# One layer with 32 routed experts on one core: results scattered to their token's place, and the down product put off behind the next gate product

## The reference, cut to what matters

```python
h2 = rms_norm(x, norm_ffn)                     # 320 tokens x 1024
grp = argmax(h2 @ w_rg + b_rg)                 # one of 4 groups
top_val, top_idx = top_k(logit_e of grp, 2)    # two of its 8 experts
y_e = (silu(xb @ w_gate[e]) * (xb @ w_up[e])) @ w_down[e]   # xb: tokens of expert e
x = x + sum over the two experts of weight * y_e
```

## Time and profile before

| | us |
|---|---|
| median of three executions | 1235.9 |
| the profiled execution | 1233.81 |
| its span | 1232.3 |
| PE busy | 1174.5 (95%) |
| DVE busy | 298.2 (24%) |
| ACT busy | 239.2 (19%) |
| POOL busy | 85.2 (7%) |

### The profile page before, as it was taken

The page is one execution under the profiler, slowest core; times in us unless marked ns, Lnnn a source line. Parts: engine busy times, 40 slices in busy tenths (PEclk is TensorE's granted clock), DMA queues, the critical chain, the costliest instruction groups (busy, mean ns, idle before and its releaser), DMA issues.

```text
span 1232.3 us, 14577 instructions
## 1 busy us (share of the span) xinstructions
PE 1174.5 (95%) x5878; PEld 647.5 (53%) x5878; DVE 298.2 (24%) x743; ACT 239.2 (19%) x497; POOL 85.2 (7%) x128
## 2 busy tenths in 40 slices
PE   6999999999899999999996999999999999899796
PEld 3477876555577777777644433333433333344243
DVE  1131033446623222131215111111111111012314
ACT  2021011334411111320012111111111111111135
POOL 0020040000112110000000000000000000001000
PEclk9999998999998888899996999999999999999998
DMA  9950194102023335355414799999999999999901
GB/s 330 274 175 1 69 166 143 47 23 69 29 81 106 107 133 200 114 205 205 156 64 190 300 414 415 414 415 415 415 414 415 414 415 415 412 415 417 334 12 43
DMA packets 77329, 288.98 MB, mean 235 GB/s; under 512 B 21587, under 2 KB 25916, under 8 KB 56732
## 3 DMA queue, kind: packets, MB, share of 16 engines
q1 hardware_dynamic: 54972, 256.67, 53.8%
q0 software_dynamic: 21920, 31.15, 8.7%
q10 hardware_dynamic: 384, 0.41, 0.1%
HBM read 276.55 MB, written 15.62 MB: 237 GB/s over the span
## 4 chain that ended last, share of the span: by engine, by line
PE 43%; DMA 13%; DVE 2%; issue 1%; ACT 1%; SPq 0%; POOL 0%; ACTq 0%; DVEq 0%
PE ps L1022 14%; DMA late<-in_w_exp_up_dram 9%; PE ps L526 8%; PE ps L1038 6%; PE ps L582 4%; PE ps L999 4%; DMA ring<-in_w_exp_up_dram 3%; PE ps L1029 2%; PE ps L1007 1%; PE ps L547 1%; PE ps L946 1%; PE ps L589 1%; PE ps L563 0%; PE ps L517 0%; PE ps L810 0%
## 5 line engine op out<-in xcount | busy, mean ns | idle before, releaser
L1022 PE MATMUL ps<-ring,reg_xh 128*64 128x512 f32 x512 | 151.1, 603 | 8.2 <-DMA late<-in_w_exp_up_dram 4.5
L1022 PE MATMUL ps<-late,reg_xh 128*64 128x512 f32 x336 | 149.2, 597 | 2.9 <-DMA reg_k<-in_w_exp_up_dram 1.7
L1853 DVE TENSOR_TENSOR reg_xh<-reg_xh,ps 64x512 f32<-64x512 f32 x32 | 22.1, 691 | 350.5 <-ACT reg_xh L1343 350.5
L1022 PEld LDWEIGHTS ps<-ring,reg_xh 128*64 128x64 f32 x512 | 49.6, 139 | 105.9 <-issue 103.6
L999 PE MATMUL ps<-reg_xh 128*64 128x512 f32 x384 | 89.6, 601 | 1.7 <-DVE reg_xh L1792 1.7
L796 PE MATMUL ps<-reg_xh,ring 128*128 128x320 f32 x256 | 83.1, 479 | 0.0
L1022 PE MATMUL ps<-reg_k,reg_xh 128*64 128x512 f32 x176 | 77.5, 593 | 0.0
L1343 ACT ACTIVATE reg_xh<-ps 64x512 f32<-64x512 f32 x32 | 34.1, 1064 | 216.2 <-PE ps L1022 216.2
L1022 PEld LDWEIGHTS ps<-late,reg_xh 128*64 128x64 f32 x336 | 45.7, 138 | 52.0 <-issue 52.0
L796 PEld LDWEIGHTS ps<-reg_xh,ring 128*128 128x128 f32 x256 | 52.6, 213 | 21.7 <-issue 7.5
L2030 POOL DMA_DIRECT2D y_rows<-reg_xh x29 | 23.2, 801 | 571.4 <-ACT reg_xh L1353 528.9
(11 more groups left out here) (363 smaller groups left out, 1499.9 us busy)
## 6 DMA issues: line engine op xcount, KB each, us to landing
ring<-in_w_exp_gate_dram SPq DMA_DIRECT2D x21, 2048.0 KB, 26.1
ring<-in_w_in_dram SPq DMA_DIRECT2D x13, 2048.0 KB, 9.0
late<-in_w_exp_gate_dram SPq DMA_DIRECT2D x11, 2048.0 KB, 25.4
reg_k<-in_w_exp_up_dram SPq DMA_DIRECT2D x11, 2048.0 KB, 30.0
ring<-in_w_exp_down_dram SPq DMA_DIRECT2D x11, 2048.0 KB, 27.8
ring<-in_w_exp_up_dram SPq DMA_DIRECT2D x11, 2048.0 KB, 30.5
reg_o<-in_w_exp_down_dram SPq DMA_DIRECT2D x11, 2048.0 KB, 28.4
late<-in_w_exp_up_dram SPq DMA_DIRECT2D x10, 2048.0 KB, 30.2
```

What stands on the lines that cost most here:

```text
L1022: last = pe.matmul(out[64 * part:64 * part + 64, :], xb[:, k, :], ws_[part][:, k, :], start=(k == 0), stop=(k == KT - 1))
```

## The change

**Results.** A zeroed `y_rows` has one row for each token and choice (2 x 320). While the router runs, DVE makes the place of each assignment (rank x 32 + expert); POOL writes the number of each target row to that place of a small table in DRAM (six indirect DMAs of 4-byte elements), loads the table back to all partitions in two DMAs, and DVE adds 0 or 1 for the column half (`slot_rows`, in the first `expert_steps`, behind the copy to `he`). Each of the 29 stores becomes an indirect scatter of 128 half rows of 2 KB, in which unused slots have an index out of bounds and are left out. At the end six plain DMAs read the rows back.

**PE's order.** For expert e: gate and up of e, gather of e+1, first half of down of e-1, row turns of e+1, second half of down of e-1, turn of e as four transposes. The last expert's down product stands behind the loop, between the first two combines. PE reads the largest count ahead of the loop. ACT's result copies and SP's loads follow this order: gate and up of e+1 are loaded ahead of down of e. DVE's order is as before, but for `slot_rows`.

```diff
+c[:, K_ROW + 3 * k + t] = 2 * (N * k + 128 * t + r)
+c[:, K_HALF] = r // 64
...
 def load_next(e, p):
     sp.wait_ge(up_done, e - 2)
     load_weights(e, 0, EXPERT_SLOTS[p][0])
     load_weights(e, 1, EXPERT_SLOTS[p][1])
+def load_down(e, p):
     sp.wait_ge(down_done, e - 2)
     load_weights(e, 2, EXPERT_SLOTS[p][2])
+load_next(3, 0)
 with sp.Fori(1, 10) as i:
     for p in range(3):
-        load_next(i * 3 + p, p)
-load_next(30, 0)
+        load_next(i * 3 + p + 1, (p + 1) % 3)
+        load_down(i * 3 + p, p)
 load_next(31, 1)
+load_down(30, 0)
+load_down(31, 1)
...
+def turn_once(out):
+    for m in range(4):
+        last = pe.transpose(out[:, SLOTS * m:SLOTS * m + SLOTS], sg[:, 128 * m:128 * m + 128], ident[64:128, 64:128])
+    return last
+def down(w_down, hb, out, rows=(0, 1, 2, 3), sg_count=None):
     w = w_down.rearrange("p (k n) -> p k n", k=4)
-    for m in range(4):
+    for m in rows:
         for c in range(2):
+            if (m, c) == (3, 1) and sg_count is not None:
+                pe.wait_ge(sg_ready, sg_count)
             last = pe.matmul(out[64 * c:64 * c + 64, :], hb[:, m, :], w[:, m, 512 * c:512 * c + 512],
                              start=(m == 0), stop=(m == 3))
     return last
 gather(sel[0], ps[:, 0, :], sel_ready, 1, gathered)
 turn_rows(xg_ready, 1, xg_turned)
-def expert(i, p, keep=None, last_one=False):
+def expert(i, p, keep=None):
     e, par, turn_no = i * 6 + p, p % 2, i * 2 + p // 3 + 1
-    w_gate, w_up, w_down = EXPERT_SLOTS[p % 3]
+    w_gate, w_up = EXPERT_SLOTS[p % 3][0:2]
+    first, last_one = keep == -1, keep == 3
     if keep is not None and keep >= 2:
         pe.wait_ge(selT_ready, keep - 1)
     pe.wait_ge(xe_ready, e + 1)
     gate_up(slots[w_gate], slots[w_up], xe[par], ps[:, 2 + par, :]).then_inc(up_done, 1)
     if not last_one:
         gather(sel[1 - par], ps[:, 1 - par, :], sel_ready, e + 2, gathered)
+    if not first:
+        before_down(i, p)
+        w_down = EXPERT_SLOTS[(p - 1) % 3][2]
+        down(slots[w_down], he[1 - par], ps[:, 5 - par, :], (0, 1))
+    if not last_one:
+        turn_rows(xg_ready, e + 2, xg_turned)
+    if first:
+        pe.wait_ge(sg_ready, 1)
     else:
-        pe.wait_ge(selT_ready, 3)
-        pe.wait_ge(ye_ready, NE + 1)
-        combine(0, ye[1]).then_inc(combined, 1)
-        combine(1, ye[0]).then_inc(combined, 1)
-    pe.wait_ge(sg_ready, e + 1)
-    turn(ps[:, 6, :]).then_inc(turned, 1)
-    if not last_one:
-        turn_rows(xg_ready, e + 2, xg_turned)
-    if keep is not None and keep < 3:
+        down(slots[w_down], he[1 - par], ps[:, 5 - par, :], (2, 3), e + 1).then_inc(down_done, 1)
+    turn_once(ps[:, 6, :]).then_inc(turned, 1)
+    if keep in (0, 1, 2):
         turn_sel(keep, 2 + par)
+def before_down(i, p):
+    e, turn_no = i * 6 + p - 1, i * 2 + (p - 1) // 3 + 1
     pe.wait_ge(he_ready, e + 1)
     pe.wait_ge(ye_ready, e + 1)
-    pe.wait_ge(chunk_in[w_down], (turn_no + uses[w_down]) * 16)
-    down(slots[w_down], he[par], ps[:, 4 + par, :]).then_inc(down_done, 1)
-with pe.Fori(0, 4) as i:
+    slot = EXPERT_SLOTS[(p - 1) % 3][2]
+    pe.wait_ge(chunk_in[slot], (turn_no + uses[slot]) * 16)
+pe.wait_ge(ranked, 1)
+most = pe.value_load(route[:, :].bitcast(I32)[0:1, 1019:1020], min_val=0, max_val=N)
+for p in range(6):
+    expert(0, p, -1 if p == 0 else None)
+with pe.Fori(1, 4) as i:
     for p in range(6):
         expert(i, p)
 for e in range(24, NE):
-    expert(e // 6, e % 6, e - STORED + 1 if e >= STORED - 1 else None, e == NE - 1)
-pe.wait_ge(ranked, 1)
-most = pe.value_load(route[:, :].bitcast(I32)[0:1, 1019:1020], min_val=0, max_val=N)
+    expert(e // 6, e % 6, e - STORED + 1 if e >= STORED - 1 else None)
+pe.wait_ge(selT_ready, 3)
+combine(0, ye[1]).then_inc(combined, 1)
+before_down(NE // 6, NE % 6)
+down(slots[EXPERT_SLOTS[(NE - 1) % 3][2]], he[1], ps[:, 5, :]).then_inc(down_done, 1)
+pe.wait_ge(ye_ready, NE + 1)
+combine(1, ye[0]).then_inc(combined, 1)
 with pe.If(most > SLOTS):
...
-def expert(i, par, first=False, last_one=False):
+def activated(i, par, last_one=False):
     e = i * 2 + par
     act.wait_ge(up_done, e + 1)
         act.wait_ge(gathered, e + 2)
         act.activation(xg, ps[:, 1 - par, :], ACT.Copy).then_inc(xg_ready, 1)
-    act.wait_ge(down_done, e + 1)
-    if last_one:
-        act.wait_ge(combined, 1)
-    elif not first:
+def result(i, par, first=False):
+    act.wait_ge(down_done, i * 2 + par + 1)
+    if not first:
         act.wait_ge(ye_out[par], i * 16)
     act.activation(ye[par], ps[:, 4 + par, :], ACT.Copy).then_inc(ye_ready, 1)
...
-expert(0, 0, True)
-expert(0, 1, True)
-with act.Fori(1, NE // 2 - 1) as i:
-    expert(i, 0)
-    expert(i, 1)
-expert(NE // 2 - 1, 0)
-expert(NE // 2 - 1, 1, last_one=True)
+activated(0, 0)
+activated(0, 1)
+result(0, 0, True)
...
+with act.Fori(2, NE // 2 - 1) as i:
+    activated(i, 0)
+    result(i - 1, 1)
+    activated(i, 1)
+    result(i, 0)
+activated(NE // 2 - 1, 0)
+result(NE // 2 - 2, 1)
+activated(NE // 2 - 1, 1, True)
+result(NE // 2 - 1, 0)
+act.wait_ge(down_done, NE)
+act.wait_ge(combined, 1)
+act.activation(ye[1], ps[:, 5, :], ACT.Copy).then_inc(ye_ready, 1)
...
+filled(dve, ("os", NB - 1))
+dve.memset(reg_pc[:, 768:1024], 0.0).then_inc(blank, 1)
+dve.memset(slot_row[:, :], NOWHERE).then_inc(blank, 1)
...
-    link(dve.tensor_scalar(i1, rk, float(SLOTS - 1), None, ALU.min))
-    link(dve.scalar_tensor_tensor(out=dest[:, 3 * k:3 * k + 3], in0=e_, scalar=float(SLOTS), in1=i1, op0=ALU.mult, op1=ALU.add))
+    link(dve.scalar_tensor_tensor(out=place[:, 3 * k:3 * k + 3], in0=rk, scalar=float(NE), in1=e_, op0=ALU.mult, op1=ALU.add))
+    if k == 1:
+        dve.tensor_copy(placei, place).then_inc(ranked, 1)
+for k, (e_, a_) in enumerate(((e1, a1), (e2, a2))):
+    rk, wm, wk = rank12[:, 3 * k:3 * k + 3], w_more[:, 3 * k:3 * k + 3], (w1_, w2_)[k]
     link(dve.tensor_scalar(stored[:, 3 * k:3 * k + 3], e_, float(STORED), None, ALU.is_lt))
-    dve.tensor_tensor(dest[:, 3 * k:3 * k + 3], dest[:, 3 * k:3 * k + 3], stored[:, 3 * k:3 * k + 3], ALU.mult)
...
-link(dve.tensor_copy(route[:, :].bitcast(U32)[:, 126:132], dest_more))
-dve.tensor_copy(desti, dest).then_inc(ranked, 1)
-dve.wait_ge(ranked, 2)
+dve.tensor_copy(route[:, :].bitcast(U32)[:, 126:132], dest_more).then_inc(ranked, 1)
+dve.wait_ge(ranked, 3)
...
+def slot_rows():
+    dve.wait_ge(row_in, 32)
+    dve.tensor_scalar(slot_row[:, :].bitcast(U32), slot_row[:, :], cst[:, K_HALF:K_HALF + 1], None, ALU.add).then_inc(ranked, 1)
...
     dve.tensor_copy(he[par].rearrange("p m n -> p (m n)"), ps[:, 6, 0:256]).then_inc(he_ready, 1)
+    if first:
+        slot_rows()
...
-with dve.Fori(0, NE // 2 - 2) as i:
+expert_steps(0, 0, first=True)
+expert_steps(0, 1)
+with dve.Fori(1, NE // 2 - 2) as i:
...
+pool.wait_ge(blank, 2)
+for t in range(5):
+    pool.dma_start(y_rows[128 * t:128 * t + 128, :].rearrange("r (q n) -> r q n", q=4),
+                   reg_pc[:, 768:1024].unsqueeze(1).broadcast_to([128, 4, 256])).then_inc(blanked, 16)
+pool.dma_start(row_of.rearrange("(s e) n -> s (e n)", e=NE), slot_row[0:SLOTS, :]).then_inc(blanked, 16)
...
-def store_rows(e, par):
+pool.wait_ge(blanked, 96)
+pool.wait_ge(cst_sem, 16)
+pool.wait_ge(ranked, 2)
+placed = route[:, :].bitcast(U32)[:, 914:920]
+for t, (_, rows) in enumerate(TILES):
+    for k in range(2):
+        col = 3 * k + t
+        pool.indirect_dma_start(row_of, bass.IndirectOffsetOnAxis(ap=placed[0:rows, col:col + 1], axis=0),
+                                cst[0:rows, K_ROW + col:K_ROW + col + 1], None,
+                                bounds_check=SLOTS * NE - 1, oob_is_err=False).then_inc(row_put, 16)
+pool.wait_ge(row_put, 96)
+for half in range(2):
+    pool.dma_start(slot_row[64 * half:64 * half + 64, :], row_of.rearrange("(s e) n -> s (e n)", e=NE)).then_inc(row_in, 16)
+pool.wait_ge(ranked, 4)
+target = slot_row[:, :].bitcast(U32)
+for e in range(STORED):
     pool.wait_ge(ye_ready, e + 3)
-    dst = first_rows[bass.ds(e, 1)].rearrange("a r n -> (a r) n")
-    pool.dma_start(halves(dst), ye[par]).then_inc(ye_out[par], 16)
-with pool.Fori(0, STORED // 2) as i:
-    for par in range(2):
-        store_rows(i * 2 + par, par)
-store_rows(STORED - 1, 0)
+    pool.indirect_dma_start(half_rows, bass.IndirectOffsetOnAxis(ap=target[:, e:e + 1], axis=0), ye[e % 2], None,
+                            bounds_check=4 * N - 1, oob_is_err=False).then_inc(ye_out[e % 2], 16)
 pool.wait_ge(ye_out[0], (STORED // 2 + 1) * 16)
 pool.wait_ge(ye_out[1], STORED // 2 * 16)
-pool.wait_ge(ranked, 2)
 pool.wait_ge(up_done, NE - 2)
-gather_rows(y_rows, 914, rows_back)
+for t, (t0, rows) in enumerate(TILES):
+    for k in range(2):
+        pool.dma_start(gath[k][t][0:rows, :], y_rows[N * k + t0:N * k + t0 + rows, :]).then_inc(rows_back[t], 16)
+pool.wait_ge(ranked, 3)
```

More of the change, by code:

```diff
@@ L49 @@
 CU, CV_, CQ, CKV, CGN, CGM = 0, 1024, 2048, 3072, 4608, 4656
-K_ID, K_UP, K_BLK, K_REP, K_IOTA, K_E, K_VALID = 0, 128, 256, 320, 384, 704, 736
-K_ALL = 737
```

(51 more changed lines are left out.)

16 lines of the change are left out of this document (8 added, 8 removed).

## The result

The changed kernel took 1259.9 us (median of four executions, 1253.6 to 1271.2); the kernel before, 1236.6 on the same chip. The ratio is 1.0202, interval 1.0126 to 1.0279. The two profiled executions stand at 1253.57 and 1233.81. Forecast were 1261 and a profiled 1259.8.

What follows compares the result with a forecast made beforehand. Before, TensorE at 14.65 us an expert was the bound, then late weights; after, TensorE at 16.09. Start 690.9, 30 periods, 1.8 and 20.6 put the third combine at 1196.0, against 1169.97: +26.0, 1261 us, range 1241 to 1283.

Steps and rivals of the forecast that it cites:

- The gap: TensorE before each gate and up: idle 1.71 us an expert from the turn's end until VectorE's gain product delivers xe.
- The turn: TensorE, each expert: eight matmul instructions of 1.03 us in all become four transposes taking 0.52 us, ends 0.26 and 0.59.
- The kept experts: VectorE, experts 28, 29 and 30: copying the turned selection is no longer hidden, 3 x 0.6 = 1.8 us.
- The end: After the loop: from expert 31's gate and up to the third combine 20.6 us, the third combine at 1196.0.
- Directly behind the second: After the loop: the third combine follows the second at once, since the count's read no longer stands before it.
- From there on the program is the same: From the third combine to the finish: same program with its inputs there, so no change in time.
- Buy nothing: Expert loop: the 5.2 MB of stores saved gain no time, as weights and used rows need 15.4 us, under 16.09.
- about 15 us: Old expert loop: all that fewer bytes could win, 0.5 us times 31 above TensorE's own 14.65.
- rows not cheaper: Scattered stores: unused rows still cost descriptors, 15.9 us an expert against 16.09, no change to the forecast; inside its case, 0.56.
- The start: Before expert 0: reading the largest count costs TensorE 0.5 us, gate and up begin at 677.6, first period 13.3 us.
- The row table: Before and in expert 0: ready at about 687, cost 0 to 7 us, taken as 0; rival of lateness, chance 0.10.
- The clock: Rival, TensorE in the loop: clock falls in the gaps, a third of them giving 1278, all 1311; chance 0.20.

Runs made afterwards that it cites:

- experiment 3: Changed kernel with the next select and gain product on VectorE moved ahead of the wait for the turn; 1217.8 us, ratio 0.9878 to the kernel before.
- experiment 4: Changed kernel with one more VectorE operation, its result unused, between select and gain product; 1294.4 us, ratio 1.0509 to the kernel before.
- experiment 7: Changed kernel with only the select moved ahead of the wait for the turn, the gain product left in place; 1242.8 us, ratio 1.0076 to the kernel before.
- experiment 2: Kernel before with only the scattered stores, row table and plain reads back added, TensorE and loads in the old order; 1218.7 us, ratio 0.9894.
- experiment 1: Kernel before with only the new order, four-transpose turn and early count, stores whole and no row table; 1251.7 us, ratio 1.0146.

## Why the prediction was right, point by point

- **The gap.** Right in place, releaser and sign: 30 gaps, ended by the gain product. Forecast 1.71, measured 1.59. The lap itself was sized well (copy at 813.01 to the end of the gain product at 814.44, 1.43 for 1.41); what was too large is the step from xe to the first matmul, 0.26, of which three laps in a row show 0.05, 0.24 and 0.12. Experiments 3, 4 and 7 take it away, lengthen it and shorten it, and the time at full clock follows their waits: 17.9 and 11.3 us of waits, 16.4 and 11.0 of time.
- **The turn** was put at 0.52; it lies 0.39 to 0.41 in the chain. With the gap that is 0.24 us an expert, and the period is 15.85 instead of 16.09. The loop came out at 510.2 us where 518.4 were forecast (677.6 to 1196.0), and this is nearly all of it. The kept experts are in it: their three periods are 16.38, 16.42 and 16.15, 1.4 over three usual ones, for 1.8.
- **The end.** From gate and up of expert 31 (1164.54) to the third combine (1185.14) are 20.60 us, forecast 20.6. "Directly behind the second" holds but for 0.40 of issue. That is less than the 2.88 of the earlier trace rows, but the read of the count was not what the 2.88 paid for: experiment 2 leaves the read in its old place and has 0.45 there, and experiment 3, with the read moved, has 1.89. What sets the amount is not explained. "From there on the program is the same" was the step that failed: the products are, but 4.5 us came in behind the last store. The experiments put them to the part with the bytes. Neither the sum nor a rival had them, and they hid more than half of the loop's error.
- **The bytes.** "Buy nothing" was right beside the gap (experiment 1, 510.3 against 510.2). The "about 15 us" of late weights in the old order were there too (experiment 2). Unused rows move nothing: the packets of POOL's queue fell from 21920 on the page before to 9936, and its 31.15 MB to 28.46, which is the forecast 5.2 MB less with 2.6 MB of zeros added. The rival "rows not cheaper" is out.
- **The start.** Gate and up of expert 0 begin at 674.94, not 677.6, but this moves with the execution: the three profiles of the changed kernel have 674.94, 680.23 and 671.09. The first period is 13.06 for 13.3. The read of the count shows no cost there.
- **The row table** did not come late. Its six writes landed in 3.3 us each and its loads in 1.9 (medians). VectorE adds the half directly behind the copy to he, with no wait between:

```profile
686.39 0.42 DVE L1916 COPY reg_xh<-ps 128x256 f32<-128x256 f32 x1 [2.52 <-PE ps L1050]
686.84 0.24 DVE L1886 TENSOR_SCALAR slot_row<-slot_row,cst 128x32 uint32<-128x32 f32 x1
```

- **The clock.** It was a rival at 0.20, priced for a third of the gaps (1278) or for all (1311). There were fewer: none of the 32 products is slow in the first profile, two in the second, six in the third. The right step would have been a term that differs between executions, 1.69 us (8.78 less 7.09) for each slow product. It is not all that differs: in the same three profiles the loop takes 510.2, 513.2 and 520.0 us, but it also starts at 674.9, 680.2 and 671.1. By the intervals of its three measurements the changed kernel is 1.3% to 3.2% over the kernel before.
- **Sum.** Forecast were +26.0. The profiled execution has +19.8: loop 8.2 under, start 2.7 under, end 4.5 over. The medians have +23.4, and later +35.8 and +28.3; at full clock the three lie within 1 us of each other. That the first of them comes so near +26.0 is in part luck: a gap and a turn that were too long were offset by an end and by clock that the sum did not have.

## What to carry to other kernels

A product on the critical engine is often the cover of another engine's lap; before it is moved, write down what runs beside it and who waits for the last operation of that lap. If a lap loses its cover, look first at its order: here the next input had waited behind a copy that only the following product needed, and two operations moved ahead of one wait turned a loss of 2% into a gain of 1.7%. Bytes are worth something only where the chain goes through a transfer, so the same bytes were worth some 15 and 0 us in the loops of the old and the new order, and 11 us of the whole time with the gap mended.

## What was not expected of the hardware

- **The longer the recurring gap, the more products ran at the lower clock.** With 1.2 us of idle ahead of each product none of 32 was at the lower pace (one trace), with 1.6 us none, two and six (three traces of the changed kernel; none and two of the order alone), with 2.2 us thirteen. Before, a single 3.5 us of idle had cost nothing, and 2.40 us had been followed by a product of 8.78. What decides in the single case is not shown. So the same gap is not priced once for all: two kernels whose waits differ by 11 us lay 25 us apart.
- **A longer end.** 8.8 us from the last store's issue to the end of the span with scatters, 4.2 without, in every trace, the same transfer landing in 2.8 in both. The cause was not isolated.
- **A scatter lands sooner than the whole store.** The issues of the changed kernel (KB where known, median us to landing), against 21.1 in the earlier trace rows:

```profile
y_rows<-reg_xh,slot_row POOLq DMA_INDIRECT x29, 8.2
```

  In experiment 2, with the DMA engines full throughout the loop, it is 6.7 us. The Trainium skill (DMA: Bandwidth & Descriptors, "Queues, rings and completion order") has each DMA engine go round the queues it has work for and drain a whole packet of one before it turns to the next. By that rule a transfer of fewer packets needs fewer turns. The direction agrees: in 200 us of the loop POOL's queue moved 7300 packets with 14 stores before and 1026 with 13 scatters after. The runs do not separate that from the smaller bytes.
- **Fewer store bytes, a higher rate.** In stretches with the engines full, 413 to 415 GB/s moved with whole stores and 420 to 424 with scattered rows. A stretch of experiment 2:

```profile
900.00:1130.00 230.00, 229.97 (x1137) 89.27 (x1135) 38.20 (x84) 35.53 (x47) 16.83 (x20) 1.00 1.01 421
```

  Weights and rows of 6.37 MB then take 15.0 to 15.2 us, and not the 15.4 of the forecast. With three experts loaded ahead, that keeps TensorE's 14.65 and 14.80 fed to the end of the loop, and its 14.15 not quite.
